# One decoder layer: norm 2 handed on tile by tile, two FFN weight blocks k-outermost, and weight and tile splits moved around three seams

## What is computed

```python
def _layer(x, c, pos, mixer, ...):
    mod = silu(c) @ w_ada + b_ada
    shift1, scale1, gate1, shift2, scale2, gate2 = split(mod, 6)
    h = rmsnorm(x, norm1_g) * (1 + scale1) + shift1
    ...                                              # projections, two kinds of attention
    mix = (g_a * (o_nsa @ w_br_nsa) + g_b * (o_dil @ w_br_dil)) @ w_out
    x = x + gate1 * mix
    h = rmsnorm(x, norm2_g) * (1 + scale2) + shift2
    f = silu(h @ w_gate) * (h @ w_up)                # D_FF = 5632
    x = x + gate2 * (f @ w_down)
```

## Time and profile before

| what | value |
|---|---|
| median of 3 runs | 2027.29 us (2025.56 to 2029.9) |
| the profiled execution's own time | 2018.94 us |
| its span, first to last instruction | 2017.1 us |
| TensorE busy | 94% (PE), 86% (weight loads) |
| DVE, ACT, POOL busy | 48%, 37%, 3% |
| mean granted TensorE clock | 0.969 of full speed |
| memory traffic | 504 MB read, 99 MB written |

### The profile page before, as it was taken

One profiled execution on the slowest core, in us unless ns is written; L12 is line 12 of the kernel. 1 busy time (PEld: TensorE's weight loads), 2 busy tenths in 40 slices (PEclk: granted clock), 3 DMA queues, 4 the chain that ended last, 5 costly groups with the idle time before them and its releaser, 6 DMA issues.

```text
span 2017.1 us, 36420 instructions
## 1 busy us (share of the span) xinstructions
PE 1887.6 (94%) x15737; PEld 1738.6 (86%) x15737; DVE 963.2 (48%) x1551; ACT 753.7 (37%) x1117; POOL 58.5 (3%) x108
## 2 busy tenths in 40 slices
PE   6988899999998988899999969999999999999997
PEld 3556799999964455899999969999999999999996
DVE  3336445555346823444546764444444444654544
ACT  2335333334434533433334334333333333533332
POOL 0000000000000000000000000000000000000000
PEclk9999999999998989799999989999999999999999
DMA  9998287999899937877878765677677676455551
GB/s 372 422 421 292 84 266 250 294 289 289 268 398 418 402 150 270 269 220 249 270 228 271 261 219 188 233 257 260 229 252 267 229 249 224 128 188 173 175 187 52
DMA packets 336262, 512.50 MB, mean 254 GB/s; under 512 B 8881, under 2 KB 310233, under 8 KB 319625
## 3 DMA queue, kind: packets, MB, share of 16 engines
q1 hardware_dynamic: 316162, 368.53, 54.8%
q0 software_dynamic: 5248, 125.73, 15.5%
q10 hardware_dynamic: 14752, 16.80, 3.2%
HBM read 504.29 MB, written 98.91 MB: 299 GB/s over the span
## 4 chain that ended last, share of the span: by engine, by line
PE 85%; DMA 7%; DVE 4%; ACT 2%; issue 1%; SPq 0%; DVEq 0%; ACTq 0%
PE bank L1176 19%; PE bank L1177 19%; PE bank L1178 19%; PE bank L858 5%; PE bank L859 5%; PE bank L860 5%; DMA piece<-in_w_ada 5%; PE bank L746 3%; PE bank L783 2%; DMA mem<-in_cache_sel_kv,runs 1%; PE bank L811 1%; DMA mem<-in_x_sample 1%; PE bank L903 1%; PE bank L772 1%; DVE piece L2132 1%
## 5 line engine op out<-in xcount | busy, mean ns | idle before, releaser
L1176 PE MATMUL bank<-piece,piece 128*128 128x264 f32 x3072 | 876.5, 285 | 32.6 <-DVE piece L2127 26.5
L1177 PE MATMUL bank<-piece,piece 128*128 128x264 f32 x3072 | 875.9, 285 | 0.0
L1178 PE MATMUL bank<-piece,piece 128*128 128x264 f32 x3072 | 875.6, 285 | 0.0
L2132 DVE TENSOR_TENSOR piece<-piece,piece 128x2048 fp32r<-128x2048 f32 (+2 forms) x216 | 440.8, 2052 | 483.6 <-ACT piece L1589 483.6
L1176 PEld LDWEIGHTS bank<-piece,piece 128*128 128x128 f32 x3072 | 581.3, 189 | 33.6 <-issue 22.6
L1178 PEld LDWEIGHTS bank<-piece,piece 128*128 128x128 f32 x3072 | 581.3, 189 | 0.0
L1589 ACT CAST piece<-piece 128x2048 fp32r<-128x2048 f32 (+2 forms) x216 | 368.9, 1715 | 567.7 <-PE bank L1178 521.3
L1177 PEld LDWEIGHTS bank<-piece,piece 128*128 128x128 f32 x3072 | 580.8, 189 | 0.0
L858 PE MATMUL bank<-piece,piece 128*128 128x264 f32 (+1 forms) x816 | 240.0, 294 | 0.0
L859 PE MATMUL bank<-piece,piece 128*128 128x264 f32 (+1 forms) x816 | 233.8, 286 | 0.0
L860 PE MATMUL bank<-piece,piece 128*128 128x264 f32 (+1 forms) x816 | 233.4, 286 | 0.0
(11 more groups left out here) (337 smaller groups left out, 1298.1 us busy)
## 6 DMA issues: line engine op xcount, KB each, us to landing
piece<-in_w_ada SPq DMA_DIRECT2D x48, 2048.0 KB, 12.4
out_s_dil<-in_cache_dil_kv POOLq DMA_DIRECT2D x64, 1023.5 KB, 6.3
piece<-in_w_in SPq DMA_DIRECT2D x50, 1024.0 KB, 8.1
piece<-in_w_gate SPq DMA_DIRECT2D x22, 2048.0 KB, 8.1
piece<-in_w_up SPq DMA_DIRECT2D x22, 2048.0 KB, 8.1
piece<-in_w_down SPq DMA_DIRECT2D x32, 1408.0 KB, 6.5
piece<-in_w_in SPq DMA_DIRECT2D x16, 2048.0 KB, 8.9
piece<-in_w_out SPq DMA_DIRECT2D x8, 2048.0 KB, 8.6
```

The lines of the kernel that those rows point to most:

```text
L1176: mm(out, w_high[:, k, :], half_tile(x_high[k]), start=(start and k == first_tile), stop=False)
L1177: mm(out, w_high[:, k, :], half_tile(x_low[k]), start=False, stop=False)
L1178: last = mm(out, w_low[:, k, :], half_tile(x_high[k]), start=False, stop=(stop and k == len(x_high) - 1))
L2132: v.tensor_tensor(half_chunk(a, k_tiles, f, CW), raw, half_chunk(buffer, k_tiles).bitcast(F32), ALU.subtract)\
```

## The change

It touches the three seams, and leaves the loops and the number of products as they are.

- *Merge to output product.* ACT casts the first 14 merged tiles as soon as the gate projections are done with the buffers (`mg_half` 46), and the last two after the second weight half; DVE makes 14 low tiles ahead of `merge(7)` and two after it.
- *Output product to FFN.* DVE does two of the four first weight splits ahead of the last two residuals and two after the normed tiles. ACT casts in the order 3, 0, 1, 2. Norm 2 takes the sample columns first and gives them the difference of their shift to the prompt's (`more_shift`); then, tile by tile, DVE scales the prompt columns, ACT adds the prompt's shift to all 264 columns and rounds in one operation (the high part), and DVE makes the low part with the shift added in the same operation. The factors `facA` are made while TensorE adds the squares, for which the products `xs8` of the residual move from `facA` to `gT`.
- *First FFN slot.* TensorE takes both halves of slot 0 together with k outermost (`both_halves`): six products per tile, into two banks. Both steps of `ff_half` come at its end.
- *FFN to down product.* ACT casts the first down weights and six hidden tiles while TensorE still does the last two half blocks of the FFN. Their high parts lie in memory that is free by then (`f_high`, `F_EARLY`). DVE splits them ahead of `hidden(10, 2)`.

```diff
-    xs8 = facA[:, 0:1, 0:B]
+    xs8 = gT[:, 0:B].unsqueeze(1)
...
-    f_high = tiles_at((hT0, 16), (oN0, 12), (spare + 2 * KD * P, 16))
+    F_EARLY = 6
+    f_high = tiles_at((spare + 2 * KD * P, 4), (ffn_high[2] + 2048, 2), (hT0, 16), (oN0, 12), (spare + 2 * KD * P + 4 * T, 10))
...
@@ block.tensor @@
+        def both_halves(s):
+
+            w_low = [half_chunk(slot_at(s), KT, f, CW) for f in range(2)]
+            w_high = [half_chunk(ffn_high[2 * s + f], KT) for f in range(2)]
+            for k in range(KT):
+                pe.wait_ge(*dve_.at("h_low", k))
+                for f in range(2):
+                    out = bank[2 * s + f][:, 0:T]
+                    mm(out, w_high[f][:, k, :], half_tile(h_high[k]), start=(k == 0), stop=False)
+                    mm(out, w_high[f][:, k, :], half_tile(h_low[k]), start=False, stop=False)
+                    last = mm(out, w_low[f][:, k, :], half_tile(h_high[k]), start=False, stop=(k == KT - 1))
+                    if k == KT - 1:
+                        last.then_inc(ff_half, 1)
...
+                if first and s == 0:
+                    pe.wait_ge(ff_low, 2)
+                    both_halves(0)
+                    continue
...
+        pe.wait_ge(ff_silu, 42)
         down(0, 0, True, True)
+        pe.wait_ge(ff_kept, 42)
         down(0, 1, True)
@@ block.scalar @@
-            if n == 0:
-                act.wait_ge(mg_half, 48)
-                for k in range(KT):
+            if n < 2:
+                if n == 0:
+                    act.wait_ge(mg_half, 46)
+                for k in (range(KT - 2), range(KT - 2, KT))[n]:
                     act.wait_ge(mg_kept, k + 1)
                     cp(half_tile(x_high[k]), mT[:, k, :]).then_inc(*act_.mark("m_high", k))
-        def ffn_first():
-
-            for n in range(4):
-                act.wait_ge(w_ld["ffn"][n // 2], 16)
-                act.wait_ge(wo_half, (14, 15, 16, 13)[n])
-                high(slot_at(n // 2), ffn_high[n], n % 2, KT, ff_high)
-        ffn_first()
-        norm("n2", 3)
-
+        for n in (3, 0, 1, 2):
+            act.wait_ge(w_ld["ffn"][n // 2], 16)
+            act.wait_ge(wo_half, (14, 15, 16, 13)[n])
+            high(slot_at(n // 2), ffn_high[n], n % 2, KT, ff_high)
+        act.wait_ge(*dve_.at("ms", "n2"))
+        A(rstd, rstd, ACT.Sqrt).then_inc(*act_.mark("root", "n2"))
+        act.wait_ge(*dve_.at("h_samples"))
         for k in range(KT):
-            act.wait_ge(*(act_.at("h", "n2", k) if k < KT - 1 else act_.at("h", "n2")))
-            act.wait_ge(*dve_.at("h", "n2"))
-            cp(half_tile(h_high[k]), hT[:, k, :]).then_inc(*act_.mark("h_high", k))
+            act.wait_ge(*dve_.at("hs", "n2", k))
+            A(half_tile(h_high[k]), hT[:, k, :], ACT.Identity, bias=modT[:, 3 * KT + k, 0:1]).then_inc(*act_.mark("h_high", k))
...
+                    if very_first and n < 4:
+                        act.wait_ge(ff_half, 85 + n)
                     high(slot_at(s), down_high[n % 4], f, KD, dn_high)
                     if very_first and f == 0:
                         for k in range(KD):
+                            if (s, k) in ((0, 0), (0, F_EARLY), (3, 0)):
+                                act.wait_ge(ff_half, 88 if k else 86)
+                                act.wait_ge(ff_kept, 44 if s else 40)
                             cp(half_tile(f_high[s * KD + k]), fT[:, s * KD + k, :]).then_inc(*act_.mark(f"f_high{s}", k))
-        act.wait_ge(ff_half, 88)
-        act.wait_ge(ff_kept, 44)
@@ block.vector @@
         wout_low(0)
+        for k in range(KT - 2):
+            merged_low(k)
         merge(7)
-        for k in range(KT):
-            dve.wait_ge(*act_.at("m_high", k))
-            low_tile(m_low[k], mT[:, k, :], x_high[k]).then_inc(*dve_.mark("m_low", k))
+        for k in range(KT - 2, KT):
+            merged_low(k)
...
+        def first_low(n):
+
+            dve.wait_ge(ff_high, min(n + 2, 4))
+            low(slot_at(n // 2), ffn_high[n], n % 2, KT, ff_low)
         for n in range(1, 16 + 3):
             if n < 16:
                 wout_low(n)
+            if n >= 17:
+                first_low(n - 17)
             if n >= 3:
...
-        for n in range(4):
-            dve.wait_ge(ff_high, n + 1)
-            low(slot_at(n // 2), ffn_high[n], n % 2, KT, ff_low)
         dve.wait_ge(wo_kept, 16)
-        norm("n2", 1, 3)
...
+        dve.wait_ge(*pe_.at("sum", "n2"))
+        mean_square("n2")
+        one_over_root("n2")
...
+        for n in range(KT + 2):
+            if n < KT:
+                v.scalar_tensor_tensor(out=hT[:, n, 0:TP], in0=xT[:, n, 0:TP], scalar=facA[:, n, 0:1],
+                                       in1=rstd[:, 0:TP], op0=ALU.mult, op1=ALU.mult).then_inc(*dve_.mark("hs", "n2", n))
+            if n >= 2:
+                k = n - 2
                 dve.wait_ge(*act_.at("h_high", k))
-                low_tile(hT0 + k * T, hT[:, k, :], h_high[k]).then_inc(*dve_.mark("h_low", k))
+                v.scalar_tensor_tensor(out=half_tile(hT0 + k * T), in0=hT[:, k, :], scalar=modT[:, 3 * KT + k, 0:1],
+                                       in1=half_tile(h_high[k]).bitcast(F32), op0=ALU.add, op1=ALU.subtract)\
+                    .then_inc(*dve_.mark("h_low", k))
+        first_low(2)
+        first_low(3)
...
                 if very_first and f == 0:
                     for k in range(KD):
+                        if (s, k) == (0, F_EARLY):
+                            hidden(10, 2)
```

More of the change, by code:

```diff
@@ L400, in program @@
     down_high = [spare, spare + KD * P, dead_consts, dead_consts + KD * P]
-    f_high = tiles_at((hT0, 16), (oN0, 12), (spare + 2 * KD * P, 16))
-    assert ffn_high[2] + 2048 <= WORDS and f_high[-1] + T <= WORDS
+    F_EARLY = 6
+    f_high = tiles_at((spare + 2 * KD * P, 4), (ffn_high[2] + 2048, 2), (hT0, 16), (oN0, 12), (spare + 2 * KD * P + 4 * T, 10))
+    assert f_high[3] + T <= ffn_high[1] + 2048 <= h_high[12] and f_high[-1] + T <= f_high[4] and f_high[5] + T <= WORDS
     assert dead_consts + 2 * KD * P <= CONST_P + 96
@@ L1233, in ffn @@
                     split_products(bank[2 * s + f][:, 0:T], slot_at(s), ffn_high[(2 * s + f) % 4], f, KT, h_high, h_low,
-                                   True, True, "h_low" if first and s == f == 0 else None).then_inc(ff_half, 1)
+                                   True, True).then_inc(ff_half, 1)
         ffn(0, True)
@@ L2168, in wout_low, with merged_low @@
             low(slot_at(s), wout_high[n % 4], f, KT, wo_low)
-        wout_low(0)
-        merge(7)
-        for k in range(KT):
+        def merged_low(k):
             dve.wait_ge(*act_.at("m_high", k))
             low_tile(m_low[k], mT[:, k, :], x_high[k]).then_inc(*dve_.mark("m_low", k))
+        wout_low(0)
+        for k in range(KT - 2):
+            merged_low(k)
+        merge(7)
+        for k in range(KT - 2, KT):
+            merged_low(k)
         def residual(j, z, gate, products, n_products, kept):
@@ L2197, in _ @@
                     v.tensor_tensor(rstd, rstd, tmp[:, 0, :], ALU.add).then_inc(*dve_.mark(*(("sum", "n2") if j == KT - 1 else ())))
-        for n in range(4):
-            dve.wait_ge(ff_high, n + 1)
-            low(slot_at(n // 2), ffn_high[n], n % 2, KT, ff_low)
         dve.wait_ge(wo_kept, 16)
-        norm("n2", 1, 3)
-        def h_tiles():
-            for k in range(KT):
-                dve.wait_ge(*act_.at("h_high", k))
-                low_tile(hT0 + k * T, hT[:, k, :], h_high[k]).then_inc(*dve_.mark("h_low", k))
+        v.scalar_tensor_tensor(out=facA, in0=modT[:, 4 * KT:5 * KT, :], scalar=1.0, in1=gT[:, KT:2 * KT].unsqueeze(2).broadcast_to([P, KT, 9]),
+                               op0=ALU.add, op1=ALU.mult).then_inc(*dve_.mark())
+        more_shift = tmp[:, 1, 0:KT * B].rearrange("p (k b) -> p k b", b=B)
+        v.tensor_tensor(more_shift, modT[:, 3 * KT:4 * KT, 1:9], modT[:, 3 * KT:4 * KT, 0:1].broadcast_to([P, KT, B]), ALU.subtract)\
+            .then_inc(*dve_.mark("fac", "n2"))
+        dve.wait_ge(*pe_.at("sum", "n2"))
+        mean_square("n2")
+        one_over_root("n2")
+        dve.wait_ge(*dve_.at("fac", "n2"))
+        hS = hT[:, :, TP:T]
+        link(v.tensor_tensor(hS, xT[:, :, TP:T], facA[:, :, 1:9], ALU.mult))
+        link(v.tensor_tensor(hS, hS, rstd[:, TP:T].unsqueeze(1).broadcast_to([P, KT, B]), ALU.mult))
+        v.tensor_tensor(hS, hS, more_shift, ALU.add).then_inc(*dve_.mark("h_samples"))
+        for n in range(KT + 2):
[4 more added lines that the diff above has]
+                k = n - 2
+                dve.wait_ge(*act_.at("h_high", k))
+                v.scalar_tensor_tensor(out=half_tile(hT0 + k * T), in0=hT[:, k, :], scalar=modT[:, 3 * KT + k, 0:1],
[3 more added lines that the diff above has]
+        first_low(3)
         def hidden(i, g):
@@ L2223, in ffn @@
                     low(slot_at(s), ffn_high[(2 * s + f) % 4], f, KT, ff_low)
-                if first and s == 0:
-                    h_tiles()
```

(1 more changed line is left out.)

## The result

The changed kernel takes 2005.4 us (median of 4 runs, 2001.16 to 2007.9); the kernel before, in the same rounds, 2028.6 us (2025.56 to 2032.75). The ratio is 0.9882, with a 95% interval of 0.9856 to 0.9909: 23.2 us less.

What follows compares the result with a forecast made beforehand. TensorE, busy 94% of the span, was taken as the bound, leaving its idle time, mainly three tile-split waits of 26.5 us. Gains of 4.0 + 13.2 + 6.2 = 23.4 us off 2027.3 gave 2003.9 us, range 2000 to 2010.

Steps and rivals of the forecast that it cites:

- The sum: Gains at the three seams added, 4.0 + 13.2 + 6.2 = 23.4 us, giving a median of 2003.9 us.
- The step that took the same difference off the median as off the profiled execution: Median lies 8.35 us above the profiled execution, none of it in the seams, so 23.4 us came off 2027.3 too.
- The signs of being wrong: Wait over 2 us before third or fourth FFN weight block, clock not back within 6 us, or FFN iterations changing length.
- Seam 1: Merge to output product: 14 of 16 merged tiles split early; gain 4.0 us (3.1 to 4.4), 0.35 us wait left.
- Seam 2, the start: Output product to FFN: TensorE starts the FFN at 1200.3 instead of 1213.66, the root waiting for the table load; gain 13.3 us.
- Seam 2, the block: First FFN slot fed tile by tile: 96 products take 13.5 us, DVE 0.81 us per tile, plus 0.1 us of wait.
- the three ends: First FFN slot: sixteen tile pairs end at 1211.5, third weight split at 1213.8, TensorE's 96 products at 1213.8, nearly coinciding.
- Seam 3: FFN to down product: 4.6 us idle and 2.4 slow clock go, 0.8 us wait comes; gain 6.2 us (5.0 to 6.9).
- Rival 1: Norm 2 block: no DVE operation starts before the former ends, 0.478 us each; 2.4 us lost, 2006.3 us; chance 0.10.
- Rival 2: Norm 2 block: short stops per tile keep TensorE at 1.2 GHz; 7.6 us lost, 2011.5 us; chance 0.05.
- Rival 3: FFN to down product: early hidden tiles don't come early, one late condition blocks them; 6.2 us less gain, 2010.1; chance 0.07.
- Rival 4: After norm 2 into the FFN loop: clock stays at 1.2 GHz; gain gone from 52 us, 2030.8 at 60; chance 0.03.

Runs made afterwards that it cites:

- seam 3 alone: Kernel before with only the early split of six hidden tiles and the first down weights: 1178.0 us from first merge product to end, 3.9 less than before.
- TensorE kept busy: Changed kernel plus 44 unread products between the sum of squares and the first FFN product: 1158.6 us from first merge product to end, 0.6 less.
- the fourth split early: Changed kernel with the fourth weight split ahead of norm 2 and half block 3 before 2: 1158.7 us from first merge product to end, 0.4 less.
- seam 1 alone: Kernel before with only the merged tiles' early casts and splits: 1179.4 us from first merge product to end, 2.5 less than before.
- seam 2 alone: Changed kernel with merge to output product and FFN to down product as before: 1169.4 us from first merge product to end, 12.5 less than before.

## Why the prediction was right

- **The sum.** 23.4 us forecast, 2003.9 us for the median. Measured 23.2 and 2005.4; in the profiles, behind the first merge product, 22.7: by parts 3.9 (up to the last output product), 13.4 less 0.3 (norm 2 and the block behind it) and 5.8 (from the third FFN block on), where the forecast had 4.0, 13.2 and 6.2. Of the 1.5 us by which the median is off, 1.3 are the fourth run of the kernel before, which moved its median from 2027.29 to 2028.6. With runs that spread over 7 us, that the medians' difference comes within 0.2 us is luck; the 22.7 are the better measure. The step that took the same difference off the median as off the profiled execution had no measurement behind it when it was made. The profiles bear it out as far as they go: the profiled execution of before started the merge at 835.21, earlier than all twelve others, nine of which started it at 842 or later. The executions without a profile can't be read in this way.
- **The signs of being wrong** did not come. No wait stands in front of the third or fourth weight block, the clock returns 4.8 us after the restart, and the FFN loop, untouched, keeps its length: 46.75 us an iteration and 502.49 us from the third FFN block to the last FFN product, before and after.
- **Seam 1**, forecast 4.0: by the gaps of the timeline 3.07 + 1.34 us have become 0.37, 4.0 us; the wait of 0.35 forecast is the 0.37. What the step left out is the clock: it took "the first seam has no slow stretch" from one execution, and in one of three it has one (seam 3 alone).
- **Seam 2, the start**, forecast 13.3: 19.88 less 6.49 is 13.4. The table load is what the root waits for, as said: it ends at 1198.96, the root runs at 1198.97.
- **Seam 2, the block**, forecast 13.5 us and 0.1 of wait: 13.92, without a wait. The pace per tile was 0.80 for 0.81; the form not in the trace, taken at 0.41 by the last norm's row, is 0.41. The slow stretch lasted 4.8 us, in its bounds of 3.7 to 5.5 and 0.7 longer than the 4.1 that the sum had taken: 0.7 x 0.45 = 0.3 of the 0.4 us that the block is over. That the three ends would nearly coincide shows in the runs with TensorE kept busy and with the fourth split early: neither a faster TensorE alone nor an earlier split alone gained more than 0.6. The three ends did not quite coincide: TensorE ends last, the weight split 0.65 us and the tiles' chain some 1.3 us before it.
- **Seam 3**, forecast 6.2: from the third FFN block to the last down product 766.87 us have become 761.07, 5.8 less, both here and with seam 3 alone. The wait of 0.8 is 0.81, and the slow stretch is gone; idle time and first slot together gave 6.1, as forecast. What the sum had at nothing is the rest of the down product: behind its first slot it takes 249.4 us in every profile with this part of the change and 249.1 in every one without. What makes these 0.35 us is not known.
- **The rivals.** Rival 1 (no operation starts before the former ends) is refuted by the rows: starts 0.40 apart, lengths of 0.48. The rule of the Trainium skill that was weighed there (VectorE: DVE Perf Modes, The DRAIN you can't avoid) does not hold for these operations; the same section adds that an operation which nothing holds starts earlier, and with that the rows agree. Rival 2's mechanism exists, but only where a tile took 1.73 us (two idle operations per pair), and did not come at 0.80 or 1.27 us a tile. Rival 3 did not come, all six conditions were met in time. Rival 4 (a long slow stretch) did not come in any of the 13 profiles; the longest stretch of busy TensorE at 1.2 GHz behind the start of the merge is 6.1 us, at seam 3 of the run with seam 1 alone.

## What to carry to other kernels

At a seam between two products, ask which engine's chain ends last there and price all three ends, TensorE's, the tile splits' and the weight splits': at norm 2 they lay within some 1.3 us of each other, so one edit more on TensorE or on the weight splits alone was worth 0 to 0.6 us, and only together they gave 1.3. Work that needs nothing new (most tiles, the next weights) belongs in front of the seam, in gaps that the trace shows as waits of the same engines. Compare profiles from a point behind which the edit acts, and count slow products apart: here the start of the merge, which no edit touched, moved by 11.7 us between profiles, and the slow stretches, one product more or less at 0.1 us each, by up to some 2 us.

## What was not expected of the hardware

- A wait of 3.2 us start to start cost the clock in one of three profiles with the same code at that place (before and seam 2 alone: granted clock 1.00; seam 3 alone: 0.50 for some 6 us). Where spare products stood behind the sum alone, a stop of 1.78 us ahead of the sum was enough: the clock fell 0.8 us after TensorE had begun to work again. With 14 more ahead of the sum it stayed at 1.00.
- The slow stretch behind the same restart at norm 2 had 16 to 23 products, 3.9 to 5.5 us, from one execution to the next, whether the idle time before it was 6 or 20 us.
- Stops of 0.4 us in 1.27 left the clock at 1.00 for 13 us; stops of 0.9 us in 1.73 made it fall and return within one block.
- ACT's first root after the table load started 0.01 us behind the load's end.
